# A streaming encoder layer with product-key retrieval on one core: two of eight one-hots go to GpSimd, and three pieces of work change their place

## What is computed

```python
q = (xb @ w_pq).reshape(128, 8, 256); q = q * rsqrt(mean(q * q) + EPS)
s1 = einsum('thd,hnd->thn', q[..., :128], sub_keys[0])   # 128 scores
s2 = einsum('thd,hnd->thn', q[..., 128:], sub_keys[1])
v1, i1 = top_k(s1, 16); v2, i2 = top_k(s2, 16)
cand = v1[..., :, None] + v2[..., None, :]
sv, si = top_k(cand, 16)                                  # 16 of 256 pairs
e = i1[si // 16] * 128 + i2[si % 16]                      # expert numbers
g = softmax(sv)
a = einsum('tkd,td->tk', peer_u[e], xb)
out = einsum('tk,tkd->td', gelu(a) * g, peer_v[e])        # 8 heads x 16 choices
```

## Time and profile before

| | |
|---|---|
| median of 3 runs | 1928.15 us (1927.27 to 1930.62) |
| the profiled execution: time, and its span | 1932.49 us, 1930.7 us |
| busy in the span | PE 1764.2, DVE 1613.6, POOL 978.8, ACT 803.5 us |
| attention and the first group's choices | 0 to 577.4 us of the span |
| turns of gates beside the second group's choices | 577.4 to 842 us |
| the blocks of experts | 842 us to the end |
| mean granted clock of TensorE | 0.956 of full speed |

### The profile page before, as it was taken

How to read it: one execution, slowest core, us unless ns; L and a number is a source line. 1 busy time by engine, 2 the same in 40 slices (tenths; PEclk the granted TensorE clock), 3 DMA queues, 4 the chain that set the end, 5 groups by cost and what they waited for, 6 DMA issues and landing times.

```text
span 1930.7 us, 28368 instructions
## 1 busy us (share of the span) xinstructions
PE 1764.2 (91%) x9239; PEld 1483.0 (77%) x9239; DVE 1613.6 (84%) x3321; ACT 803.5 (42%) x1314; POOL 978.8 (51%) x779
## 2 busy tenths in 40 slices
PE   6999899888959877569999999999999999999998
PEld 4883454677628776459989998999899989998997
DVE  5205463489879799989999999999999999999999
ACT  4312562344316655434344344434444443444343
POOL 0004000024340023267777777777777777777773
PEclk7999999898879988779999999999999999999999
DMA  6110303233114444289999999999999999999996
GB/s 250 44 64 2 131 1 125 93 125 106 70 51 146 171 146 138 81 322 416 416 392 400 400 392 392 401 408 392 395 411 392 392 405 399 398 395 409 393 393 272
DMA packets 169006, 517.87 MB, mean 268 GB/s; under 512 B 18129, under 2 KB 51857, under 8 KB 164849
## 3 DMA queue, kind: packets, MB, share of 16 engines
q0 software_dynamic: 73728, 268.47, 34.9%
q1 hardware_dynamic: 70448, 223.46, 30.5%
q10 hardware_dynamic: 24768, 25.17, 3.8%
HBM read 486.20 MB, written 30.84 MB: 268 GB/s over the span
## 4 chain that ended last, share of the span: by engine, by line
PE 76%; DVE 17%; ACT 4%; issue 2%; DMA 1%; SPq 0%; ACTq 0%; DVEq 0%
PE ps L1297 28%; PE ps L1313 9%; PE ps L1315 9%; PE ps L1314 9%; PE ps L1146 3%; DVE asel L1585 2%; DVE bsel L1578 2%; PE ps L985 2%; PE ps L987 2%; PE ps L986 2%; PE ps L1185 1%; PE ps L1234 1%; DVE wpql L1337 1%; PE ps L1105 1%; PE ps L1012 1%
## 5 line engine op out<-in xcount | busy, mean ns | idle before, releaser
L628 POOL DMA_INDIRECT ubuf<-in_peer_u,ix x256 | 387.0, 1512 | 156.2 <-POOL ix L673 109.1
L628 POOL DMA_INDIRECT vbuf<-in_peer_v,ix x256 | 397.6, 1553 | 78.9 <-issue 77.7
L1313 PE MATMUL ps<-hh,uh 128*128 128x384 f32 x1024 | 346.8, 339 | 17.8 <-DVEq L1706 17.8
L1315 PE MATMUL ps<-hh,ul 128*128 128x384 f32 x1024 | 345.8, 338 | 0.0
L1314 PE MATMUL ps<-hl,uh 128*128 128x384 f32 x1024 | 344.4, 336 | 0.0
L1718 DVE SCALAR_TENSOR_TENSOR ubuf<-ubuf,h2Y 128x1024 f32<-128x1024 f32 x256 | 302.6, 1219 | 0.8 <-issue 0.7
L931 ACT ACTIVATE vh<-vb 128x1024 fp32r<-128x1024 f32 x128 | 136.0, 1062 | 304.2 <-PE ps L1297 295.9
L1297 PE MATMUL ps<-vl,acth 128*128 128x512 f32 x774 | 243.1, 395 | 0.0
L1297 PE MATMUL ps<-vh,actl 128*128 128x512 f32 x774 | 242.5, 394 | 0.0
L1297 PE MATMUL ps<-vh,acth 128*128 128x512 f32 x774 | 242.5, 394 | 0.0
L1313 PEld LDWEIGHTS ps<-hh,uh 128*128 128x128 f32 x1024 | 193.9, 189 | 24.2 <-issue 18.6
(11 more groups left out here) (367 smaller groups left out, 2961.6 us busy)
## 6 DMA issues: line engine op xcount, KB each, us to landing
ub<-in_peer_uT SPq DMA_DIRECT2D x130, 512.0 KB, 6.7
vb<-in_peer_v SPq DMA_DIRECT2D x129, 512.0 KB, 6.5
gbuf<-gate_matrix SPq DMA_DIRECT2D x68, 384.0 KB, 8.2
gate_matrix<-stage ACTq DMA_DIRECT2D x12, 2048.0 KB, 7.8
wpqX<-in_wpq SPq DMA_DIRECT2D x8, 1024.0 KB, 5.3
wpqY<-in_wpq SPq DMA_DIRECT2D x8, 1024.0 KB, 5.0
w_oX<-in_w_o SPq DMA_DIRECT2D x4, 1024.0 KB, 7.9
kTs<-in_past_k SPq DMA_DIRECT2D x8, 512.0 KB, 3.9
```

The lines of the kernel that those rows point to most:

```text
L628: nc.gpsimd.indirect_dma_start(out=dst[slot][:, e, :], out_offset=None, in_=t_in[table], in_offset=bass.IndirectOffsetOnAxis(ix[:, slot, e ...
L1313: mm(ps[:, 6 + slot, 0:NTD], uh[slot][:, k], hh[:, k], start=(k == 0), stop=False)
L1315: last = mm(ps[:, 6 + slot, 0:NTD], ul[s][:, k], hh[:, k], start=False, stop=(k == KD - 1))
```

## The change

Four things change. The third tile's output product on TensorE moves behind the last stream's values, next to the fourth's, and VectorE's last copies of the first group move into the choices of the last pair. The comparing instruction on VectorE and ScalarE's two multiplications are gone from each turn: GpSimd now forms the last two tokens' tables itself, by `last_two(k)`, in its own in-order stream. The list of stages follows each head: queries and scores of head h+1 come behind the choices of head h, where two heads were ahead, with eight turns ahead of head 0 instead of eleven. The halves of the first group's query weights are runs of 512 input features instead of 128 query columns.

```diff
         def later():
-            behind = {("start", 0): 2, ("normed", 3): 1, ("normed", 4): 2, ("queries", 0): 2, ("scores", 0): 1,
-                      ("queries", 1): 2, ("scores", 1): 1}
-            stages = [("start", 0), ("normed", 3), ("normed", 4),
-                      ("queries", 0), ("scores", 0), ("queries", 1), ("scores", 1)]
+            behind = {("start", 0): 2, ("normed", 3): 1, ("normed", 4): 1, ("queries", 0): 2, ("scores", 0): 2}
+            stages = [("start", 0), ("normed", 3), ("normed", 4), ("queries", 0), ("scores", 0)]
...
-                if h + 2 < PH:
-                    stages += [("queries", h + 2), ("scores", h + 2)]
+                if h + 1 < PH:
+                    stages += [("queries", h + 1), ("scores", h + 1)]
                 behind[stages[-1]] = 6
...
+            def last_two(k):
+                if k == 0:
+                    pool.wait_ge(selT_copied, 3)
+                if k >= RING:
+                    pool.wait_ge(sel_used, 2 * (k - RING) + 2)
+                for j in range(PART - 2, PART):
+                    tok = k * PART + j
+                    ins = nc.gpsimd.tensor_scalar(asel[:, k % RING, j], iota[:], i1T[:, tok:tok + 1], gT[:, tok:tok + 1],
+                                                  ALU.is_equal, ALU.mult)
+                ins.then_inc(asel_pool, 1)
+
+            for stage_, x in later():
+                if stage_ == "gates":
+                    if x < TURNS:
+                        last_two(x)
+                elif stage_ == "pair":
+                    second_keys(1, x)
+                    if x < PH // 2 - 1:
+                        first_keys(1, x)
...
-            def scale_two(k):
-                act.wait_ge(asel_ones, k + 1)
...
-            def round_weights(h, c):
+            def round_weights(h, half):
...
-                feats = slice(c * P, (c + 1) * P)
-                A(wpq_hi[:, :, feats], GR[0].wpq[h % 2][:, :, feats], ACT.Copy).then_inc(wpq_rounded, 1)
+                ks = slice(half * KD // 2, (half + 1) * KD // 2)
+                A(wpq_hi[:, ks], GR[0].wpq[h % 2][:, ks], ACT.Copy).then_inc(wpq_rounded, 1)
...
                     if half == 1:
-                        pe.wait_ge(asel_scaled, k + 1)
+                        pe.wait_ge(asel_pool, k + 1)
...
             sample_values(DB - 2)
-            project_out(TD)
             turn_rows(DB - 2)
...
             last.then_inc(up_done, 1)
+            project_out(TD)
             project_out(TD + 1)
             turn_choices()
...
-                V.tensor_tensor(asel[:, q, PART - 2:PART], iota[:].unsqueeze(1).broadcast_to(pair_),
-                                i1T[:, first + PART - 2:first + PART].unsqueeze(2).broadcast_to(pair_),
-                                ALU.is_equal).then_inc(asel_ones, 1)
...
-                if h == PH:
-                    copy_out(ALL - 1)
-                    dve.wait_ge(up_done, 1)
...
                     if h < PH:
                         normalise(FIRST + h)
+                    else:
+                        copy_out(ALL - 1)
+                        some(items, 8)
+                        dve.wait_ge(up_done, 1)
```

More of the change, by code:

```diff
@@ L843, in gap_exponentials @@
                 A(GR[g].gap[:], GR[g].gap[:], ACT.Exp).then_inc(gap_exp, 1)
-            def scale_two(k):
-                act.wait_ge(asel_ones, k + 1)
-                for j in range(PART - 2, PART):
-                    tok = k * PART + j
-                    ins = A(asel[:, k % RING, j], asel[:, k % RING, j], ACT.Copy, scale=gT[:, tok:tok + 1])
-                ins.then_inc(asel_scaled, 1)
             def evict(k):
@@ L1171, in queries @@
                     pe.wait_ge(pq_copied, PH + h - 1)
+                if g == 0:
+                    for half in range(2):
+                        if half == 1 and between is not None:
+                            between()
+                        pe.wait_ge(wpq_split, 2 * h + half + 1)
+                        for c in range(2):
+                            for k in range(half * KD // 2, (half + 1) * KD // 2):
+                                feats = slice(c * P, (c + 1) * P)
+                                hi, lo = wpq_hi[:, k, feats], wpq_lo[h % 2][:, k, feats]
+                                mm(out[:, c], hi, hh[:, k], start=(k == 0), stop=False)
+                                mm(out[:, c], hi, hl[:, k], start=False, stop=False)
+                                last = mm(out[:, c], lo, hh[:, k], start=False, stop=(k == KD - 1))
+                        last.then_inc((wpq_used, pq_done)[half], 1)
+                    return
                 for c in range(2):
-                    if c == 1 and between is not None:
-                        between()
                     for k in range(KD):
-                        feats = slice(c * P, (c + 1) * P)
-                        if g == 0:
-                            if k == 0:
-                                pe.wait_ge(wpq_split, 2 * h + c + 1)
-                            hi, lo = wpq_hi[:, k, feats], wpq_lo[h % 2][:, k, feats]
-                            mm(out[:, c], hi, hh[:, k], start=(k == 0), stop=False)
-                            mm(out[:, c], hi, hl[:, k], start=False, stop=False)
-                            last = mm(out[:, c], lo, hh[:, k], start=False, stop=(k == KD - 1))
-                        else:
-                            last = mm(out[:, c], x.wpq[h % 2][:, k, feats], x.h2T[:, k, :],
-                                      start=(k == 0), stop=(k == KD - 1))
-                    if g == 0 and c == 0:
-                        last.then_inc(wpq_used, 1)
+                        last = mm(out[:, c], x.wpq[h % 2][:, k, c * P:(c + 1) * P], x.h2T[:, k, :],
+                                  start=(k == 0), stop=(k == KD - 1))
                 last.then_inc(pq_done, 1)
@@ L1569, in _ @@
             keys = iota[:].unsqueeze(1).broadcast_to(part)
-            pair_ = [P, 2, NK]
             def make_gates(k):
```

31 lines of the change are left out of this document (12 added, 19 removed).

## The result

The changed kernel takes 1911.54 us (median of 3 runs, 1910.99 to 1913.54) against 1928.15: a ratio of 0.9909, 95% interval 0.9895 to 0.9922. That is 16.6 us less by the medians, where I had forecast 8.2. Beside the experiments the same kernel ran once more, with 0.9914 (0.9901 to 0.9928). Its profiled execution has a span of 1909.2 us and took 1910.99.

A forecast was written before the change was run, and what follows sets the result against it. VectorE was taken to bound the stretch before the last phase, with a wait ahead; -4.6 - 6.9 + 4.3 - 1.5 + 0.5 = -8.2 gave 1924.3 us for the profiled execution, 1920 for the median, range 1908 to 1941.

The forecast's parts named there:

- the likeliest case: The forecast's own case for the whole kernel: 1914 to 1926 us, given 45%.
- One-hots to GpSimd: In the turns: GpSimd's instruction takes 0.43 us, costs VectorE 0.25; a turn 3.15 instead of 3.01, +4.3 over 31 turns.
- the dear rival: In the turns: the shared port costs more than the edit frees; at 0.8 us per instruction 1951; above 1934, 25%.
- duration less 0.18: Price to VectorE of a GpSimd instruction on the shared port: 0.22 us for one of 0.40.
- The cheap rival: In the turns: GpSimd's instruction lasts 0.30 us, costs 0.1; a turn 2.87, time 1909.5; under 1914, 18%.
- Third tile's product later: Ahead of the turns: turn 0 begins at 572.8 instead of 577.36, -4.6 us.
- The new order: Stages behind turn 0: with head 0's queries after three turns, waits of some 10 us become 1.2 and 0.7; -6.9 us.
- my walk: Step through the new stage order from turn 0 to the end of head 1's choices: 66.3 against 73.2 us, -6.9.
- the small waits: VectorE's remaining waits for TensorE's gate products in the turns, hidden by the ring and VectorE's choices: -1.5 us.
- GpSimd's queue: Behind the second pair: decoding, transfers and one-hots wait for each other, delaying one turn; +0.5 us.
- Weights by runs: First group's query weights by runs of features: same elements, instructions and products, 0 us.
- the head gives nothing: Ahead of turn 0: decoding or transposes stay late, -4.6 is lost, 1925; with a somewhat dearer port 1926 to 1934, 12%.

The follow-up runs named there:

- a_three: The changed kernel, but GpSimd forms three of the eight one-hots and VectorE five; ratio 0.9966 to the kernel before.
- b_order: The kernel before with only the list of stages changed to follow each head; ratio 0.9973 to the kernel before.
- a_gather: The changed kernel with GpSimd's index copies and four indirect transfers six turns later, at the sixth head's choices; ratio 0.9881 to the kernel before.
- a_split: The changed kernel with two turns between queries and scores for heads 1 to 7, four behind the scores; ratio 0.9905 to the kernel before.
- b_head: The kernel before with only the third tile's output product moved later, together with VectorE's last copies; ratio 0.9974 to the kernel before.
- b_pool: The kernel before with only GpSimd forming the last two one-hots of each turn, in the old order of stages; ratio 0.9990.

## Why the prediction was wrong in its size

The direction and the range held (1911.5 lies in 1908 to 1941). The size didn't, twice what I forecast, and the likeliest case was the wrong one.

**One-hots to GpSimd: this is the step that failed.** "A turn becomes 3.15 us": it became 2.73. The two numbers behind it were both wrong, in opposite directions. The instruction lasts 0.866 us and not 0.43; it costs VectorE 0.03 us and not 0.25. The first error alone would have been the dear rival, 1951. The part was to cost 7.2 us (48 turns at 0.14, and 0.5 for the queue); it brought 2 us alone and 4 among the others, 4.0 and 5.4 by the traces of the stretch. What failed in the reasoning was the carry from one row: the earlier trace rows is an addition of two full tensors, and I took its price, as duration less 0.18, for an instruction with one tensor. The experiments give 0.03 to 0.15 us in the median for four kinds, against the duration; only where a product on GpSimd is under way as `bsel` begins does the row's price return, 0.22 and 0.28 us. Alone, the part's 2 us aren't told apart from nothing.

By the rule that I had cited as speaking against the change (the Trainium skill, "SBUF — State Buffer", section "Who interferes with whom"), the second engine to issue would be blocked for the whole instruction, 0.866 us. I had left out the section's condition: it exempts a VectorE instruction that has one input and doesn't run in a mode that uses both ports, and no run here shows in which mode the six run. No trace of a GpSimd scalar instruction shows such a block on VectorE. The other direction does show: GpSimd's instruction that started with `bsel` lasted up to 1.9 us instead of 0.87, `bsel`'s 1.2 us being in its way. There the same section, which says that a VectorE instruction with two inputs in SBUF contends with GpSimd's reads, agrees. So it is GpSimd that pays: 1.9 and 0.87 make 2.77 us a turn, just about VectorE's 2.73. Its first fourteen took 19.07 us back to back, 2.72 a turn:

```profile
568.69 19.07 POOL L651 TENSOR_SCALAR asel<-iota,i1T,gT 128x128 f32<-128x128 f32 x14 [7.11 <-ACT i2T L910]
```

With three (a_three) it no longer fits.

**The cheap rival** had the right time (1909.5) and the right turn within 0.14 (2.87), for a wrong reason: GpSimd's instruction was to last 0.30 like its copies. What it leaned on (the Trainium skill, "GPSIMD Engine Reference", section "Engine selection": one input runs roughly at line rate) isn't borne out for instructions with scalars: 0.866 us, or 0.601 with one operation, for 128 elements, where VectorE takes 0.33.

**Third tile's product later.** Predicted -4.6; it gave 6.4 to 6.6 us by the traces, from the key scores to turn 0, and in time 5.0 alone and some 8 among the others. The mechanism was right: the decoding was hidden (it ended at 561.6), and tile 4's normalisation came right ahead of turn 0. Turn 0 began at 568.62 and not at 572.8. Of these 4.2 us, 2.3 lie ahead of the part: VectorE's copy came at 524.18 and not at 526.5, since this execution was 2.2 us ahead of before's already at 502 us. The rest are sizes: 30.8 us for two products that took 29.5, 4.65 for the normalisation that took 4.35, and the 0.3 behind it. The 2 us for a lower clock were right: from the copy to the end of the up-projection it took 10.6 us instead of 8.5, at a granted clock of 0.50, the lower level (1.2 GHz), in place of a mean of 0.78. Ahead of that TensorE had been busy for 0.7 us of 10 now, and for 10.0 before. The rows give length, busy PE, PEld, DVE, ACT, POOL, clock, DMA, GB/s, first before, then now:

```profile
532.43:540.91 8.48, 5.34 (x53) 3.66 (x53) 3.53 (x20) 1.13 (x3) 0.00 (x0) 0.78 0.31 101
524.18:534.79 10.61, 7.49 (x54) 5.01 (x54) 8.34 (x47) 1.13 (x3) 0.00 (x0) 0.50 0.22 78
```

The two products, and the start of tile 4's normalisation:

```profile
534.72 29.50 PE L1150 MATMUL ps<-w_oY,oTY 128*128 128x512 f32 x64
...
564.27 1.22 DVE L1472 TENSOR_TENSOR x2Y<-x2Y,ps 128x1024 f32<-128x1024 f32 x1 [6.56 <-PE ps L1150]
```

**The new order.** At turns of 3.01 us my walk and the small waits come to -10.8 (-6.9, 17 turns of 0.14, -1.5); alone it gave 5.2, by the trace 6.2. I had written that TensorE's queries and scores hide behind the ring and VectorE's choices. They don't quite: TensorE first works off the turns that stand in the ring, and only then begins the queries. VectorE meets them in the fourth turn behind a head's choices, with 1.3 and 3.0 us in b_order and 2.1 and 2.6 in the changed kernel.

**GpSimd's queue.** Predicted +0.5 behind the second pair, where one turn would wait. a_gather shows 2.82 and 2.78 us, some 5 us in the time. I had put the one-hots of the next turn directly behind the transfers in before's timing, at 761.6, and found VectorE's fifth turn just there; with turns of 2.7 us VectorE comes sooner. The second wait came 22 us later and is TensorE's lateness: it took up the next head's queries at 743.76, in a_gather at 736.88, and GpSimd had stood idle for 9.23 us when the wait ended. This one also goes when queries and scores stand apart (0.32 us in a_split).

**Weights by runs.** Predicted 0, measured 0.

**The rival "the head gives nothing"** fell with b_head. **The dear port** fell with the turn of 2.73 us, here and in b_pool.

So the errors of the order (-10.8 for some -6) and of the queue (0.5 for 5) hid a part of the error of the port, which is why the forecast missed by 8 us and not by more.

## What to carry to other kernels

What an instruction on one engine costs the other isn't its duration: price it by a row of the same kind, with the same number of tensor inputs, or keep the whole range open. When work goes to an idle engine, add up that engine's own cycle with the blocked time in it, and look at everything in its in-order queue; transfers that it issues belong at a place where the consumers of its new work are busy with something else. And time freed on the bounding engine shows only when the ring and the other engines' order let it through: GpSimd's one-hots took 13.5 us off VectorE and shortened its stretch by 4.0 us in one order and by 5.4 in the other, and three of eight lost 10 us. Last, measure a part from a common point close ahead of it: 2.2 of the 8.7 us by which turn 0 came forward had nothing to do with the change.

## What the runs showed of the hardware that I had not expected

GpSimd's comparing instruction with two scalars for each partition needs 0.78 us for 128 elements with VectorE idle and 0.87 beside it, 0.60 with one operation and one scalar, and a product of two tensors 0.40 to 0.46: the form with fewer tensor inputs is the slower one. The two scalar forms cost VectorE less (0.03 and 0.06 us) than the two products (0.09 and 0.15).

Which engine waits goes by the start and by the kind. A product that follows directly on another and starts 0.04 us ahead of `bsel` holds it up by 0.22 or 0.28 us; one that starts 0.04 us behind `bsel` takes 1.44 us itself instead of 0.39. GpSimd's scalar instruction is the one that waits in either case, but for the three longer `bsel` named above. It takes up to 1.9 us when it starts together with `bsel`, and in a_three even when it starts 0.07 us ahead, while `bsel` keeps its 1.21:

```profile
668.58 4.57 POOL L651 TENSOR_SCALAR asel<-iota,i1T,gT 128x128 f32<-128x128 f32 x3
...
668.65 1.21 DVE L1582 TENSOR_TENSOR bsel<-iota,i2T 128x1024 f32<-128x1024 f32 x1
```

Why the price goes that way the runs don't settle; that GpSimd holds the way to memory only for a short part of its longer instructions would fit all four, but nothing here shows it directly.
